# New lags and rates in the table that orders a hybrid DeltaNet and Conformer layer on one core

## The chip, the cores and the metric

The kernel runs on one core of a Trainium2 chip. A core has five engines that run side by side, each through its own queue of instructions in order: TensorE (PE, matrix products, with its weight loads PEld), VectorE (DVE), ScalarE (ACT), GpSimd (POOL) and SyncE (SP, which here only issues transfers). They wait for each other by semaphores. The metric is the device time of one execution in microseconds (us).

## The reference

One layer works on 256 latent tokens and 256 context tokens of width 2048, in fp32.

```
p  = h @ w_in           # latent tokens: q, k, v, beta/g, z, conformer a and gate
pc = hc @ w_in[:, :STATE_END]            # context tokens: k, v, beta/g are what counts
q, k, v = silu(depthwise_conv5(...)); q, k = l2_normalize(q), l2_normalize(k)
m     = strict_lower((k beta) k^T * decay);  t_inv = inverse(eye + m)     # per chunk
v_new = u - w @ state;  state = state * cd + k_dec^T @ v_new              # scan, both directions
mix = [rms_norm(o) * silu(z) , silu(layer_norm(depthwise_conv31(a * sigmoid(gate))))]
x   = x + g1 * rms_norm(mix @ w_out)
x   = x + g2 * rms_norm(swiglu(...))                                      # FFN
```

There are 8 heads of 128 columns, and the scans of the latent tokens start from the states that the context tokens leave.

## The kernel before

Each fp32 product is made of three products of rounded halves (hi by hi, lo by hi, hi by lo). Weights come in units of 512 KB into a ring of 4 (`raw`); ACT rounds a unit to `w_hi` (step `hi`, line 858) and DVE makes the rest `w_lo` (step `lo`, lines 1280 and 1247). A unit of `w_in` is used in two halves of 12 matmuls each (step `mm`, line 1700); this half is the beat of the program.

The program has three stages: modulation columns and first projections (up to about 130 us), the mixer (130 to 900 us), and the FFN (from there to the end). The mixer is written as one list of steps, `PLAN`, made by `make_plan`. Every engine walks the same list and takes the steps that are its own, so the list sets the order in every queue. In the skeleton of that list stand the halves of the projections in a fixed order (`STREAM`: for each pair of heads k and v of the context, a and g of the latent, later k, v, q, z of the latent). After each half the planner counts one slot on, and `beside` puts other steps in:

- three queues, `solve` (`solved`), `state` (`state_steps`) and `ready` (`keys_ready`, `queries_ready`). The head of a queue is placed when the steps that it names are at least so many slots back (`lag`); the tuple `(2, x)` reads "two slots after x". With an empty list it comes one slot after the chunk before it;
- `soon`: steps so many slots after the end of a projection (`evacuation`): the 5-tap convolution of k, v and q (`tap2` on ACT, `tapa` and `taps` on DVE, lines 973 and 1386), its SiLU (`csilu`, ACT, line 980), and its transpose (`nat`);
- `late`: the 31-tap convolution of a pair of channel tiles, 15 steps `dw` (DVE, line 1558, 4 instructions or more each), and behind the last of them the layer norm (`lnm`, `cen`, `lnv`, `lva`, `lnr`, `lnn`, `mix_lo`).

For each of eight pairs of heads (4 of the context, 4 of the latent) `solved` inverts a triangular matrix: `seed` (PE, line 1885) needs `yone` (DVE, writes `pi`, line 1431), then six levels of `z`, `zc`, `xy`, `xadd` (PE, ACT, PE, DVE: lines 1897, 858, 1907, 1444), the last `xadd` (DVE, writes `xyi`, line 1449), then a Newton step: `nr` (PE, lines 1916 and 1920) needs `xyi`, `nrr` (DVE, writes `zi`, line 1456), `nx` (PE, line 1928), `xf` (DVE, line 1469). `keys_ready` normalizes the keys (`kn`, DVE, line 1400) and transposes them (`kT`, PE, the helper line 1706, reads `kn`), makes decay factors (`dec`, `edec`) and the matrix (`gk`, `mneg`). `state_steps` runs the scan: `vn`, `vnc`, `st`, `ks`, `o`. The aux steps of PE share two PSUM banks: such a step waits until the reader of the one two before has taken its result away. `hi` and `lo` of later units are tied to the levels by `splits_ahead`: inside the solve `hi` follows `zc`, `lo` follows `xadd`.

Of the kernel before, what the change touches and what calls it, by code (L numbers as in the profile page):

```python
# [53 lines left out]
LEVELS = 7  # L54
# [13 lines left out]
GATE_STEPS = ["bac", "baT", "bsig", "ny", "nex", "nln", "gg", "pref", "eall", "nbe"]  # L68
# [6 lines left out]
PAIRS = [(CTX, p) for p in range(NP)] + [(LAT, p) for p in range(NP)]  # L75
# [4 lines left out]
def solved(m):  # L80

    s, p = PAIRS[m]
    old = [(*PAIRS[m - 1], t) for t in range(NT)] if m else []
    ch = []
    if m:
        ch = [([("nr", o) for o in old] + [("nrr", o) for o in old], [(2, ("xadd", (*PAIRS[m - 1], LEVELS - 1)))]), ([("nx", old[0])], [(1, ("nr", old[1]))]),
              ([("xf", old[0]), ("nx", old[1])], []), ([("xf", old[1])], [])]
    ch.append(([("yone", (s, p))], [(1, ("mk", (s, p, 0)))]))
    ch.append(([("seed", (s, p)), ("xadd", (s, p, 0)), ("mk", (s, p, 1))], []))
    for l in range(1, LEVELS):  # L90
        ch.append(([("z", (s, p, l))], [(2, ("xadd", (s, p, l - 1)))]))
        ch.append(([("zc", (s, p, l)), ("xy", (s, p, l)), ("xadd", (s, p, l))] + (
            [("mk", (s, p, l + 1))] if l + 1 < LEVELS else [("mlo", (s, p, t)) for t in range(NT)]), []))
    return ch

def last_solved():

    both = [(*PAIRS[-1], t) for t in range(NT)]
    return [([("nr", k) for k in both] + [("nrr", k) for k in both], [(2, ("xadd", (*PAIRS[-1], LEVELS - 1)))]), ([("nx", k) for k in both], [(1, ("nr", both[1]))]),  # L100
            ([("xf", k) for k in both], [])]

# [15 lines left out]
def queries_ready(p):  # L119

    t0, t1 = (LAT, p, 0), (LAT, p, 1)
    return [([("nsq", (LAT, "q", p)), ("nrt", (LAT, "q", p)), ("gm", (*t0, 1))], [(1, ("natc", ("q", LAT, p)))]),
            ([("nrc", (LAT, "q", p)), ("kn", (LAT, "q", p)), ("qdec", (p, 1))], []),
            ([("qT", (p, 0)), ("qTc", (p, 0)), ("dec", (*t0, 1)), ("edec", (*t0, 1)), ("gm", (*t1, 1))], [(2, ("kn", (LAT, "q", p)))] + (
                [(1, ("o", (p - 1,)))] if p else [])),
            ([("qT", (p, 1)), ("qTc", (p, 1)), ("qdec", (p, 2)), ("qk", (p, 0)), ("gq", (p, 0)), ("attn", (p, 0))], [(2, ("qT", (p, 0)))]),
            ([("dec", (*t1, 1)), ("edec", (*t1, 1)), ("qT", (p, 2)), ("qTc", (p, 2))], [(2, ("qT", (p, 1)))]),
            ([("qk", (p, 1)), ("gq", (p, 1)), ("attn", (p, 1))], [])]

def state_steps(m):

    s, p = PAIRS[m]
    ch = []
    for i in range(NT):
        first, last = (s == CTX and i == 0), (s == LAT and i == 1)
        ch.append(([("vb", (s, p, i))] + ([] if last else [("kd", (s, p, i))]) + (
            [] if first else [("ks", (s, p, i)), ("r", (s, p, i))]), [] if i else [(0, ("xf", (s, p, 1)))]))
        ch.append(([("vn", (s, p, i)), ("vnc", (s, p, i))], [(4, ("vb", (s, p, i)))]))
        if not last:  # L140
            ch.append(([("st", (s, p, i)), ("stc", (s, p, i))], [(2, ("vn", (s, p, i)))]))
    if s == LAT:
        ch.append(([("o", (p,)), ("oc", (p,)), ("osq", (p,)), ("ort", (p,))], [(1, ("attn", (p, 1)))]))
        ch.append(([("orc", (p,)), ("on", (p,))], [(3, ("o", (p,)))]))
        ch.append(([("oT", (p,)), ("ym", (p,)), ("mix_hi", (p,)), ("mix_lo", (p,))], [(2, ("on", (p,)))]))
    return ch

def norm_chunks():

    ch = [[("lnm", ()), ("cen", ())], [("csq", (0,))]]
    ch += [[("lnv", (i,)), ("lva", (i,))] + ([("csq", (i + 1,))] if i < 3 else []) for i in range(4)]
    ch += [[("lsd", ()), ("lnr", ()), ("lnn", ())]]
    ch += [[("lny", (i,)), ("mix_hi", (NP + i,)), ("mix_lo", (NP + i,))] for i in range(4)]
    return ch

def evacuation(cu):

    what, s, p = cu  # L160
    if what in "kvq":
        return [("tap2", cu), ("tapa", cu)], [(2, [("taps", cu)]), (6, [("csilu", cu)]), (6, [("nat", cu), ("natc", cu)])], []
    if what == "z":
        return [("zsilu", cu)], [], []
    if what == "a":
        return [], [], []
    return [("sg", (p,)), ("u", (p,))], [], [[("dw", (p, n))] for n in range(NDW)]
# [6 lines left out]
def turn_steps(q, s):  # L174

    return [(k, (s, kp)) for kp in range(4 * q, 4 * q + 4) for k in ("hf", "hhi", "hlo")]

def make_plan():
# [5 lines left out]
    def put(steps):  # L185
        plan.extend(steps)
        for x in steps:
            placed[x] = slot[0]

    def unit(u, halves=1, beside=lambda: None):  # L190
        plan.extend([("hi", (u,)), ("lo", (u,))])
        for half in range(halves):
            plan.append(("mm", (u, half)))
            beside()

    solve = [x for m in range(len(PAIRS)) for x in solved(m)] + last_solved()
    state = [x for m in range(len(PAIRS)) for x in state_steps(m)]
    ready = [x for m in range(NP + 1) for x in keys_ready(m)]
    for p in range(NP):
        ready += (keys_ready(NP + 1 + p) if p < NP - 1 else []) + queries_ready(p)  # L200
    queues = [solve, state, ready]
    since = [0, 0, 0]
    soon = []
    late = []
    slot = [0, 0, 0]

    def advance():

        slot[0] += 1
        for n, queue in enumerate(queues):  # L210
            if queue and slot[0] > since[n] and all(
                    x in placed and slot[0] - placed[x] >= lag for lag, x in queue[0][1]):
                put(queue.pop(0)[0])
                since[n] = slot[0]
# [9 lines left out]
    def beside():  # L224

        advance()
        if soon and slot[0] >= soon[0][0]:
            follow(soon.pop(0)[1])
        if late and (slot[0] % 2 == 1 or 1 * len(late) > slot[2] - slot[0]):
            put(late.pop(0))  # L230

    def follow(steps):
        for kind, key in steps:
            m = PAIRS.index(key[1:]) if kind == "nat" else 0
            if kind == "nat" and m >= (2 if key[0] in "kv" else NP + 2):
                s, p = PAIRS[m - 2]
                until({"k": ("st", (s, p, 1 if s == CTX else 0)), "v": ("vb", (s, p, 1)), "q": ("qT", (p, 2))}[key[0]])
        put(steps)

    def gates(n):  # L240
        for grp, j in mr[:n]:
            if grp and j == 0:
                plan.extend([("mcol", (grp - 1,)), ("mcc", (grp - 1,))])
            plan.append(("mrm", (grp, j)))
            if j == KT - 1:
                plan.append(("mrc", (grp,)))
        del mr[:n]
# [3 lines left out]
    for n in range(NMOD):  # L251
# [14 lines left out]
        if n >= NMOD // 2 + 4 and n % 2 == 0 and early:  # L266
            cu, g = early.pop(0)
# [6 lines left out]
    for n, cu in enumerate(STREAM):  # L274
        if cu == ("z", LAT, NP - 1):
            gates(len(mr))
            plan.extend([("mcol", (MR - 1,)), ("mcc", (MR - 1,))])
        rest = [c[0] for c in STREAM[n:]]
        slot[2] = slot[0] + 8 * (rest.index("g") + 1 if "g" in rest else 4)
        for g in range(2 if cu in EARLY else 0, 4):  # L280
            unit(("win", cu, g), 2, beside)
            done += 1
            gates(MR * KT * done // total - (MR * KT - len(mr)))
            if n == 0:
                plan.extend(turn_steps(1, LAT)[6 * (g - 2):6 * (g - 2) + 6])
        now, then, later = evacuation(cu)
        put(now)
        soon += [(slot[0] + wait, steps) for wait, steps in then]
        late += later
        if cu == ("g", LAT, 3):  # L290
            late += norm_chunks()
        if n in (1, 5):
            s = n // 4
            unit(("ba", s))
            put([(x, (s,)) for x in GATE_STEPS[:7]])
            soon.append((slot[0] + 7, [(x, (s,)) for x in GATE_STEPS[7:]]))
            soon.sort(key=lambda x: x[0])
    for c, kg in WO_FIRST:
        if kg < 4:
# [1790 lines left out]
```

## Time and profile before

| | us |
|---|---|
| median of 3 runs | 1712.98 |
| lowest, highest | 1710.34, 1717.55 |
| the profiled execution | 1717.55 |
| its span, first to last instruction | 1715.8 |
| PE busy | 1576.0 (92%) |
| DVE busy | 1040.8 (61%) |
| ACT busy | 769.3 (45%) |

Idle time in front of an instruction is put down to whoever ended it. From 900 us on the FFN keeps PE busy nearly all the time, and no step there is in the list that is changed.

### The profile page before, as it was taken

What the parts mean: (1) busy time and instruction counts of PE and PEld (TensorE: products, weight loads), DVE (VectorE), ACT (ScalarE), POOL (GpSimd) and SP (SyncE); (2) the same over time, 40 slices, a digit from 0 to 9 for tenths busy, and PEclk for the clock granted to TensorE, in tenths of its full rate; (3) what the DMA queues carried; (4) which work ended last, traced back from release to release, by engine and by line L of the source; (5) the groups of instructions that cost most, each with busy time, mean ns of one, the idle gap of its engine ahead of it and who ended that gap; (6) DMA issues with size and microseconds to landing.
All of it is one profiled execution on the core that took longest, in us unless ns stands there. A gap on an engine that the chain in (4) does not pass through costs nothing.

```text
span 1715.8 us, 25102 instructions
## 1 busy us (share of the span) xinstructions
PE 1576.0 (92%) x9317; PEld 1316.5 (77%) x9317; DVE 1040.8 (61%) x1436; ACT 769.3 (45%) x1036; POOL 222.0 (13%) x236
## 2 busy tenths in 40 slices
PE   4778889898989789999999799999999999999997
PEld 0356879787878788888878688888888888888785
DVE  1245888898798647575555645444545455677553
ACT  5435353434343654646544544444444444343332
POOL 2000222222222332424400000000000000000000
PEclk9899999899999999999999899999999999999999
DMA  9975535555554345464355366665656665988553
GB/s 360 400 283 168 176 130 196 169 170 166 172 177 156 124 146 192 141 206 151 113 182 193 101 191 190 188 192 185 193 185 190 188 188 178 328 315 311 211 181 114
DMA packets 182786, 334.58 MB, mean 195 GB/s; under 512 B 14707, under 2 KB 80355, under 8 KB 181794
## 3 DMA queue, kind: packets, MB, share of 16 engines
q1 hardware_dynamic: 182002, 330.89, 57.7%
q0 software_dynamic: 688, 2.39, 0.5%
q8 instruction: 63, 1.03, 0.2%
q14 instruction: 33, 0.26, 0.0%
HBM read 331.15 MB, written 2.10 MB: 194 GB/s over the span
## 4 chain that ended last, share of the span: by engine, by line
PE 74%; DVE 10%; DMA 6%; issue 5%; ACT 3%; POOL 1%; SPq 1%; DVEq 0%; ACTq 0%; POOLq 0%
PE PS L1700 61%; DMA first<-in_w_mod_dram 5%; DVE w_lo L1280 2%; DVE sil L1386 2%; PE PS L1907 2%; PE PS L1706 2%; DVE cacc L1558 2%; PE PS L1955 2%; PE PS L2000 2%; PE PS L1855 1%; PE PS L1897 1%; PE PS L1920 1%; DMA raw<-in_w_mod_dram 1%; PE PS L1793 1%; DVE mn L1420 1%
## 5 line engine op out<-in xcount | busy, mean ns | idle before, releaser
L858 ACT ACTIVATE w_hi<-raw 128x1024 fp32r<-128x1024 f32 x426 | 447.7, 1056 | 546.2 <-PE PS L1700 455.0
L1247 DVE TENSOR_TENSOR w_lo<-raw,w_hi 128x1024 fp32r<-128x1024 f32 x264 | 323.2, 1225 | 330.0 <-ACT w_hi L858 330.0
L1700 PE MATMUL PS<-w_hi,h_hi 128*128 128x512 f32 x704 | 274.8, 390 | 0.0
L1700 PE MATMUL PS<-w_hi,h_lo 128*128 128x512 f32 x704 | 274.0, 389 | 0.0
L1700 PE MATMUL PS<-w_lo,h_hi 128*128 128x512 f32 x704 | 274.0, 389 | 0.0
L1280 DVE TENSOR_TENSOR w_lo<-raw,w_hi 128x1024 fp32r<-128x1024 f32 x162 | 202.5, 1258 | 80.8 <-ACT w_hi L858 80.8
L1700 PE MATMUL PS<-h_hi,w_hi 128*128 128x256 f32 (+1 forms) x784 | 238.6, 304 | 2.3 <-DVE sil L1386 2.3
L1700 PE MATMUL PS<-h_lo,w_hi 128*128 128x256 f32 (+1 forms) x784 | 224.3, 286 | 0.0
L1700 PE MATMUL PS<-h_hi,w_lo 128*128 128x256 f32 (+1 forms) x784 | 224.0, 286 | 0.0
L1700 PEld LDWEIGHTS PS<-h_hi,w_hi 128*128 128x128 f32 (+1 forms) x784 | 151.5, 193 | 37.6 <-issue 30.9
L1700 PEld LDWEIGHTS PS<-w_hi,h_lo 128*128 128x128 f32 x704 | 132.1, 188 | 27.6
L1700 PEld LDWEIGHTS PS<-w_lo,h_hi 128*128 128x128 f32 x704 | 132.2, 188 | 27.1
L1700 PEld LDWEIGHTS PS<-w_hi,h_hi 128*128 128x128 f32 x704 | 132.2, 188 | 27.0
L1700 PEld LDWEIGHTS PS<-h_lo,w_hi 128*128 128x128 f32 (+1 forms) x784 | 151.8, 194 | 0.9
L1700 PEld LDWEIGHTS PS<-h_hi,w_lo 128*128 128x128 f32 (+1 forms) x784 | 151.3, 193 | 0.1
L1700 PE MATMUL PS<-w_hi,act_hi 128*128 128x512 f32 x352 | 140.4, 399 | 0.0
L1700 PE MATMUL PS<-w_hi,act_lo 128*128 128x512 f32 x352 | 139.5, 396 | 0.0
L1700 PE MATMUL PS<-w_lo,act_hi 128*128 128x512 f32 x352 | 139.5, 396 | 0.0
L1558 DVE SCALAR_TENSOR_TENSOR cacc<-ub,vcol,cacc 128x196 f32<-128x196 f32 (+14 forms) x240 | 121.1, 565 | 0.2
L807 POOL TENSOR_TENSOR mkl<-kc,lvl 128x512 fp32r<-128x512 f32 x56 | 78.8, 1408 | 170.3 <-PE PS L1897 159.3
L1700 PE MATMUL PS<-hc_hi,w_hi 128*128 128x256 f32 (+1 forms) x272 | 83.8, 308 | 11.7 <-DVE sil L1386 3.7
L1444 DVE TENSOR_TENSOR gh<-PS,side 128x1024 fp32r<-128x1024 f32 x48 | 58.6, 1221 | 52.2 <-PE PS L1907 49.8
(314 smaller groups left out, 2396.0 us busy)
## 6 DMA issues: line engine op xcount, KB each, us to landing
raw<-in_w_in_dram SPq DMA_DIRECT2D x128, 512.0 KB, 3.9
raw<-in_w_mod_dram SPq DMA_DIRECT2D x96, 512.0 KB, 5.1
raw<-in_w_gate_dram SPq DMA_DIRECT2D x88, 512.0 KB, 3.5
raw<-in_w_up_dram SPq DMA_DIRECT2D x88, 512.0 KB, 3.5
raw<-in_w_down_dram SPq DMA_DIRECT2D x88, 512.0 KB, 4.3
first<-in_w_mod_dram SPq DMA_DIRECT2D x64, 512.0 KB, 9.4
raw<-in_w_out_dram SPq DMA_DIRECT2D x32, 512.0 KB, 4.2
gin<-in_w_mod_dram SPq DMA_DIRECT2D x32, 512.0 KB, 5.5
```

The lines of the kernel that those rows point to most:

```text
L807: pool.tensor_tensor(mkl[:, :, :, :].rearrange("p t h c -> p (t h) c"), kc[:, :, :, :].bitcast(F32).rearrange("p t h c -> p (t h) c"), bc( ...
L858: act.activation(out_ap, in_ap, ACT.Copy).then_inc(S[kind], 1)
L1247: dve.tensor_tensor(w_lo[:, slot, :], raw[:, (R0 + n) % RING, :], w_hi[:, slot, :].bitcast(F32), ALU.subtract).then_inc(S["lo"], 1)
L1280: dve.tensor_tensor(lo, raw[:, at_ring[u] % RING, 0:sz], hi.bitcast(F32), ALU.subtract).then_inc(done, 1)
L1386: ins = dve.scalar_tensor_tensor(out=o, in0=pr[:, T * h + a + off:T * h + b + off], scalar=vcol[:, col:col + 1], in1=o, op0=ALU.mult, op1= ...
L1444: dve.tensor_tensor(gh[:, :, :, :, :].rearrange("p a t h c -> p (a t h) c"), grown.rearrange("p a (n c) -> p (a n) c", c=P), bc(side[:, l, ...
L1558: ins = dve.scalar_tensor_tensor(out=dst, in0=src, scalar=vcol[:, col:col + 1], in1=dst, op0=ALU.mult, op1=ALU.add)
L1700: ins = pe.matmul(out_ap, a[i], b[j], start=start and n == 0, stop=stop and n == 2, skip_group_check=grouped)
L1706: ins = pe.transpose(PS[:, bank_, P * n:P * (n + 1)], src, ident[:, :])
L1907: ins = pe.matmul(PS[:, b, P * n:P * (n + 1)], a, m, start=False, stop=True, skip_group_check=True)
L1955: ins = pe.matmul(PS[:, b, P * n:P * (n + 1)], a, m, start=True, stop=True)
L2000: ins = pe.matmul(PS[32 * tile:32 * tile + 1, 3, :], csil[:, LAT, j:j + 1], raw[:, n % RING, 512 * h:512 * (h + 1)], start=j == 0, stop=j ...
```

## The change

Six lags and two rates of the planner get other numbers. The step `nr` no longer asks for two slots behind the last `xadd`, and `nx` asks for two behind `nr` instead of one; the same in `last_solved`. The second transposition of the queries and `st` lose their lag. `on` asks for two slots behind `o` instead of three. `csilu` comes 4 slots behind the end of its projection instead of 6. The second half of the gate steps (`pref`, `eall`, `nbe`) comes 4 slots behind instead of 7. The `late` steps are placed in every slot, not in every second, once twice their number is more than the slots left. No computation is added or taken away, and the order of the weight transfers stays.

```
@@ solved, last_solved
-        ch = [([("nr", o) ...], [(2, ("xadd", (*PAIRS[m - 1], LEVELS - 1)))]), ([("nx", old[0])], [(1, ("nr", old[1]))]),
+        ch = [([("nr", o) ...], []), ([("nx", old[0])], [(2, ("nr", old[1]))]),
...
@@ queries_ready
-            ([("qT", (p, 1)), ("qTc", (p, 1)), ... ("attn", (p, 0))], [(2, ("qT", (p, 0)))]),
+            ([("qT", (p, 1)), ("qTc", (p, 1)), ... ("attn", (p, 0))], []),
@@ state_steps
-            ch.append(([("st", (s, p, i)), ("stc", (s, p, i))], [(2, ("vn", (s, p, i)))]))
+            ch.append(([("st", (s, p, i)), ("stc", (s, p, i))], []))
...
-        ch.append(([("orc", (p,)), ("on", (p,))], [(3, ("o", (p,)))]))
+        ch.append(([("orc", (p,)), ("on", (p,))], [(2, ("o", (p,)))]))
@@ evacuation
-        return [...], [(2, [("taps", cu)]), (6, [("csilu", cu)]), (6, [("nat", cu), ("natc", cu)])], []
+        return [...], [(2, [("taps", cu)]), (4, [("csilu", cu)]), (6, [("nat", cu), ("natc", cu)])], []
@@ make_plan
-        if late and (slot[0] % 2 == 1 or 1 * len(late) > slot[2] - slot[0]):
+        if late and (slot[0] % 2 == 1 or 2 * len(late) > slot[2] - slot[0]):
...
-            soon.append((slot[0] + 7, [(x, (s,)) for x in GATE_STEPS[7:]]))
+            soon.append((slot[0] + 4, [(x, (s,)) for x in GATE_STEPS[7:]]))
```

What it moves is seen in the queues. First DVE, from the last `xadd` of the second pair of heads (`xyi`) to the normalized keys of the third (`kn`). `cacc` is the 31-tap convolution, `sil` the 5-tap one, `zi` is `nrr`, `xf_ctx` is `xf`. Before:

```order
L1558 SCALAR_TENSOR_TENSOR cacc<-ub,vcol,cacc 128x4x59 x2
L1558 SCALAR_TENSOR_TENSOR cacc<-ub,vcol,cacc 128x4x60 x2
L1449 TENSOR_TENSOR xyi<-PS,tri 128x2x512 x2
L1280 TENSOR_TENSOR w_lo<-raw,w_hi 128x1024 x2
L1558 SCALAR_TENSOR_TENSOR cacc<-ub,vcol,cacc 128x4x61 x2
L1558 SCALAR_TENSOR_TENSOR cacc<-ub,vcol,cacc 128x4x62 x2
L1456 TENSOR_TENSOR zi<-PS,ident 128x512 x2
```

The same place now:

```order
L1449 TENSOR_TENSOR xyi<-PS,tri 128x2x512 x2
L1280 TENSOR_TENSOR w_lo<-raw,w_hi 128x1024
L1558 SCALAR_TENSOR_TENSOR cacc<-ub,vcol,cacc 128x4x59 x2
L1558 SCALAR_TENSOR_TENSOR cacc<-ub,vcol,cacc 128x4x60 x2
L1456 TENSOR_TENSOR zi<-PS,ident 128x512 x2
```

One step of the convolution that stood ahead of `xyi` now stands behind it. Some rows further on the keys stood behind the 5-tap convolution of the values; before:

```order
L1386 SCALAR_TENSOR_TENSOR sil<-PS,vcol,sil 128x254
L1280 TENSOR_TENSOR w_lo<-raw,w_hi 128x1024
L1469 TENSOR_TENSOR xf_ctx<-PS,xyi 128x512
L1394 RECIPROCAL rstd<-rtmp 128x4
L1400 TENSOR_TENSOR kn<-kn,rstd 128x512
```

and now they stand ahead of it:

```order
L1469 TENSOR_TENSOR xf_ctx<-PS,xyi 128x512
L1558 SCALAR_TENSOR_TENSOR cacc<-ub,vcol,cacc 128x4x63 x4
L1469 TENSOR_TENSOR xf_ctx<-PS,xyi 128x512
L1394 RECIPROCAL rstd<-rtmp 128x4
L1400 TENSOR_TENSOR kn<-kn,rstd 128x512
L1386 SCALAR_TENSOR_TENSOR sil<-PS,vcol,sil 128x254
```

The second place is DVE in the solve of the fourth pair of heads, where the last of the four 31-tap convolutions runs (from its fourth level to the next `xadd`, `gh`). Before there is one step `dw` (two rows) between `gh` and `gh` or two:

```order
L1444 TENSOR_TENSOR gh<-PS,side 128x1024
L1280 TENSOR_TENSOR w_lo<-raw,w_hi 128x1024
L1558 SCALAR_TENSOR_TENSOR cacc<-ub,vcol,cacc 128x4x53 x2
L1558 SCALAR_TENSOR_TENSOR cacc<-ub,vcol,cacc 128x4x54 x2
L1558 SCALAR_TENSOR_TENSOR cacc<-ub,vcol,cacc 128x4x55 x2
L1558 SCALAR_TENSOR_TENSOR cacc<-ub,vcol,cacc 128x4x56 x2
L1444 TENSOR_TENSOR gh<-PS,side 128x1024
```

and now there are three:

```order
L1444 TENSOR_TENSOR gh<-PS,side 128x1024
L1280 TENSOR_TENSOR w_lo<-raw,w_hi 128x1024
L1558 SCALAR_TENSOR_TENSOR cacc<-ub,vcol,cacc 128x4x55 x2
L1558 SCALAR_TENSOR_TENSOR cacc<-ub,vcol,cacc 128x4x56 x2
L1280 TENSOR_TENSOR w_lo<-raw,w_hi 128x1024
L1558 SCALAR_TENSOR_TENSOR cacc<-ub,vcol,cacc 128x4x57 x2
L1558 SCALAR_TENSOR_TENSOR cacc<-ub,vcol,cacc 128x4x58 x2
L1558 SCALAR_TENSOR_TENSOR cacc<-ub,vcol,cacc 128x4x59 x2
L1558 SCALAR_TENSOR_TENSOR cacc<-ub,vcol,cacc 128x4x60 x2
L1444 TENSOR_TENSOR gh<-PS,side 128x1024
```

The `late` steps of the fourth convolution end 12 slots earlier (slot 147, not 159), and the layer norm behind them with them.

## Rows read from the trace of the kernel before

**Rows 1.** The page's first and second part: busy us; granted clock in 40 slices.
```profile
PE 1576.0 (92%) x9317; PEld 1316.5 (77%) x9317; DVE 1040.8 (61%) x1436; ACT 769.3 (45%) x1036; POOL 222.0 (13%) x236
PEclk9899999899999999999999899999999999999999
```
**Rows 2.** Busy time, 130 to 900 us: PE, PEld, DVE, ACT, POOL, PEclk, DMA, GB/s.
```profile
130.00:900.00 770.00, 698.87 (x5239) 622.34 (x5238) 559.80 (x929) 371.24 (x575) 212.76 (x209) 0.96 0.50 163
```
**Rows 3.** Waits of PE, 130 to 900 us: total us, times, longest.
```profile
PE PS L1916 <- issue: 9.8, 3, 4.0
PE PS L1706 <- DVE kn L1400: 7.9, 6, 1.8
PE PS L1885 <- DVE pi L1431: 7.2, 5, 2.9
PE PS L1916 <- DVE e_ L1405: 6.0, 2, 4.0
...
PE PS L1872 <- ACT qTs L858: 2.3, 3, 0.8
```
**Rows 4.** Timeline of PE in the first pair: start, us, instruction [idle before].
```profile
152.26 0.66 PE L1706 MATMUL PS<-ident,sil 128*128 128x128 f32 x4 [1.67 <-ACT sil L980]
...
156.62 0.35 PE L1700 MATMUL PS<-h_hi,w_hi 128*128 128x256 f32 x1 [2.27 <-DVE sil L1386]
...
177.80 0.36 PE L1700 MATMUL PS<-hc_hi,w_hi 128*128 128x256 f32 x1 [2.49 <-DVE ub L1538]
```
**Rows 5.** The chain of waits, second pair's last level: start, us, what.
```profile
303.42 3.07 PE PS L1700 x24
306.49 3.30 issue
```
**Rows 6.** Timeline of DVE at the same place.
```profile
305.83 1.59 DVE L1558 SCALAR_TENSOR_TENSOR cacc<-ub,vcol,cacc 128x236 f32<-128x236 f32 x4
307.34 2.35 DVE L1449 TENSOR_TENSOR xyi<-PS,tri 128x1024 fp32r<-128x1024 f32 x2
```
**Rows 7.** Timeline of DVE and PE at the third pair's keys.
```profile
322.89 2.04 DVE L1386 SCALAR_TENSOR_TENSOR sil<-PS,vcol,sil 128x254 f32<-128x254 f32 x4 [3.69 <-ACT sil L973]
...
326.78 0.69 DVE L1400 TENSOR_TENSOR kn<-kn,rstd 128x512 f32<-128x512 f32 x1
...
327.53 0.66 PE L1706 MATMUL PS<-ident,kn 128*128 128x128 f32 x4 [1.38 <-DVE kn L1400]
```
**Rows 8.** The same engines at the fourth pair's seed.
```profile
429.10 2.53 DVE L1558 SCALAR_TENSOR_TENSOR cacc<-ub,vcol,cacc 128x224 f32<-128x224 f32 x4
431.56 0.67 DVE L1431 SCALAR_TENSOR_TENSOR pi<-mkl,nid_r 128x512 fp32r<-128x512 f32 x1
...
432.28 1.11 PE L1885 MATMUL PS<-nid_r,pi 128*128 128x128 f32 x4 [2.85 <-DVE pi L1431]
```
**Rows 9.** Busy time of all engines in two stretches of the fourth convolution.
```profile
454.30:504.70 50.40, 44.47 (x351) 39.89 (x351) 45.36 (x75) 21.67 (x34) 13.56 (x13) 0.97 0.54 178
504.70:541.00 36.30, 34.11 (x255) 31.04 (x254) 33.62 (x64) 13.85 (x20) 10.54 (x9) 0.95 0.51 164
```
**Rows 10.** Busy time of line 1558 alone in the same: DVE, PEclk, DMA, GB/s.
```profile
454.30:504.70 50.40, 18.00 (x36) 0.97 0.54 178
504.70:541.00 36.30, 11.84 (x24) 0.95 0.51 164
```
**Rows 11.** Timeline of DVE and PE at the fifth pair's last level.
```profile
577.71 1.75 DVE L1579 RECIPROCAL cx<-cx 128x256 f32<-128x256 f32 x1
579.49 2.29 DVE L1582 TENSOR_TENSOR cacc<-cacc,cx 128x2048 f32<-128x2048 f32 x1
...
582.26 0.77 PE L1916 MATMUL PS<-xyi,nid_r 128*128 128x512 f32 x1 [4.00 <-DVE e_ L1405]
```
**Rows 12.** Busy time around two long waits of PE.
```profile
308.00:319.00 11.00, 9.21 (x42) 9.05 (x42) 9.98 (x16) 1.44 (x2) 0.00 (x0) 0.53 0.62 200
...
581.00:589.00 8.00, 6.74 (x31) 6.57 (x32) 4.87 (x9) 3.51 (x6) 0.00 (x0) 0.57 0.24 68
```

More of the change, by code:

```diff
@@ L85, in solved @@
     if m:
-        ch = [([("nr", o) for o in old] + [("nrr", o) for o in old], [(2, ("xadd", (*PAIRS[m - 1], LEVELS - 1)))]), ([("nx", old[0])], [(1, ("nr", old[1]))]),
+        ch = [([("nr", o) for o in old] + [("nrr", o) for o in old], []), ([("nx", old[0])], [(2, ("nr", old[1]))]),
               ([("xf", old[0]), ("nx", old[1])], []), ([("xf", old[1])], [])]
@@ L99, in last_solved @@
     both = [(*PAIRS[-1], t) for t in range(NT)]
-    return [([("nr", k) for k in both] + [("nrr", k) for k in both], [(2, ("xadd", (*PAIRS[-1], LEVELS - 1)))]), ([("nx", k) for k in both], [(1, ("nr", both[1]))]),
+    return [([("nr", k) for k in both] + [("nrr", k) for k in both], []), ([("nx", k) for k in both], [(2, ("nr", both[1]))]),
             ([("xf", k) for k in both], [])]
@@ L125, in queries_ready @@
                 [(1, ("o", (p - 1,)))] if p else [])),
-            ([("qT", (p, 1)), ("qTc", (p, 1)), ("qdec", (p, 2)), ("qk", (p, 0)), ("gq", (p, 0)), ("attn", (p, 0))], [(2, ("qT", (p, 0)))]),
+            ([("qT", (p, 1)), ("qTc", (p, 1)), ("qdec", (p, 2)), ("qk", (p, 0)), ("gq", (p, 0)), ("attn", (p, 0))], []),
             ([("dec", (*t1, 1)), ("edec", (*t1, 1)), ("qT", (p, 2)), ("qTc", (p, 2))], [(2, ("qT", (p, 1)))]),
@@ L161, in evacuation @@
     if what in "kvq":
-        return [("tap2", cu), ("tapa", cu)], [(2, [("taps", cu)]), (6, [("csilu", cu)]), (6, [("nat", cu), ("natc", cu)])], []
+        return [("tap2", cu), ("tapa", cu)], [(2, [("taps", cu)]), (4, [("csilu", cu)]), (6, [("nat", cu), ("natc", cu)])], []
     if what == "z":
```

## The prediction

> **What bounds the kernel now.** First the page: PE is busy 1576.0 us of the 1715.8, 92%, and the next engine, DVE, 61% [rows 1]. The slices say where the rest is: up to slice 22 or so, about 950 us, the granted clock dips to 8 tenths now and then; later it hardly does [rows 1]. The steps that the change touches all lie in the mixer, so I asked for the busy time from 130 to 900 us: PE 698.87 of 770 us, so 71 us idle, and a mean clock of 0.96 [rows 2]. With two levels, 1.2 and 2.4 GHz, 0.04 missing means 8% of the stretch, 62 us, at the lower one, and half of that, about 31 us, is lost to it. These 71 and 31 us, 102 together, are all that an order can win here; the work is the same before and after. Then the waits of PE in that stretch: PE waits mostly for DVE, a few us at a time [rows 3]. The line 1916 rows are `nr` after the last level, 9.8 and 6.0 us in five waits; the trace names "issue" or `e_` as releaser, but `nr` needs `xyi`, and the timeline shows it: `xyi` (307.34, 2.35 us) ends at 309.7, and the wait that began at 306.49 and lasted 3.30 us ends at 309.8 [rows 5, 6]. `xyi` itself was late because DVE had a convolution step of 1.59 us ahead of it [rows 6]. So what counts is in which order DVE takes its work where it has a backlog, and how much PE work stands between a step and its reader.
>
> **The start (pairs one and two).** Three waits of PE: 1.67 us for the SiLU of the first keys, 2.27 us for `taps`, 2.49 us for `u` [rows 4]. `csilu` two slots earlier is done before the first gate steps on ACT, so the 1.67 us go; what is late next is `taps` of the values, which DVE starts about 0.7 us earlier, so of the 2.27 us wait 1 us more is waited (the 1.67 us saved only bring PE there earlier): gain 1.0. The early `pref` (1.4 us of PE, moved from behind the matrix to ahead of it) lets `mneg`, POOL's `kc` and `seed` come about 2.5 us earlier; `u` follows its projection instead of `yone`. Gain 2. Together **-3**, between 0 and -6.4 (all three waits gone).
>
> **Keys.** `kT` waits for `kn` six times, 7.9 us [rows 3]. At the third pair DVE takes `tapa` (2.04 us, itself 3.69 us late), `lo` and `xf` ahead of `kn`; `kT` starts 0.06 us after `kn` ends [rows 7]. In the new order `kn` stands ahead of that `tapa`, so it is some 4 to 5 us earlier, while `kT` moves only one slot, about 2.8 us with its aux work. These waits vanish where DVE has the keys' norms in time; one of the six lies in the stretch priced below (1.5 us). Of the other 6.4 us I take **-5.5**; bounds 0 and -6.4.
>
> **Seeds.** Five waits for `pi`, 7.2 us [rows 3]. At the fourth pair DVE did 2.53 us of convolution ahead of `pi` [rows 8]; now `yone` stands ahead of that step, and `seed` moves one slot. 2.53 against one half of 1.53 us (24 matmuls 3.07 us, so 12 take 1.53 [rows 5]): about 1 us per pair plus what the faster `mneg` gives. Four pairs: **-3.5**; bounds +1 and -7.2.
>
> **The Newton step.** `nr` moves one slot ahead relative to its level, so PE has one half, 1.53 us, less to do before it. DVE gives `xyi` earlier by the step that now stands behind it, 1.59 us at the second pair [rows 6], nothing at the first. `nx` keeps its place, so no new wait after it. At the first pair `kk` stands right behind `nr` and needs its bank, which `nrr` frees only after `lo`, `taps` and `lo` on DVE: a new wait, from 0 to 3 us. Four pairs with a wait now: 4 x 1.53 = 6.1 against about 3 won: **+3**; bounds -2 and +9. Behind the waiting `nr` are all products of PE; ACT and DVE then idle for their next projection (the 3.69 us in [rows 7]).
>
> **The fourth convolution.** Its 15 steps take 18.00 us (36 instructions, 9 steps) in 454 to 505 us and 11.84 us (6 steps) in 505 to 541 us [rows 10]. All 15 now fall into the first stretch, where DVE was already busy 45.36 of 50.4 us [rows 9]: 45.4 + 11.8 = 57.2 us, 6.8 us more than the stretch has. PE waits for it at `z` of the fifth level and at `nr`. Add 1.2 us for the sums over channels, which need a bank there: **+8**; bounds +2 (if PE's own idle time and low clock in the stretch, about 7 us, take it up) and +11.
>
> **Where it is given back.** At the fifth pair DVE did the reciprocal and the scaling of the layer norm, 1.75 + 2.29 us, right ahead of `nr`'s needs, and PE waited 4.00 us, then ran at a clock of 0.57 for 8 us [rows 11, 12]: at 0.57, 6.9 of 8 us at 1.2 GHz, 3.4 us lost. Now the norm is done before. The wait, the 3.4 us, and 1.6 us of small waits of the norm's own steps and of `mix_lo`, 9.0 in all; one new bank wait of about 1 us behind `nr`: **-8**; bounds 0 and -10.
>
> **The rest.** The second transposition of queries: three waits of `qk` for `qTc`, 2.3 us in all [rows 3]; the new order has a `dec` and a transposition next to each other in their place: **+1**, bounds -2 and +5. `st` right behind `vn`, `on` and the later `pref` cost nothing: one half of PE, 1.53 us, covers the copy between. The clock: by [rows 12] a wait of 3.30 us was followed by 11 us at 0.53, so each long wait that goes or comes takes 2 to 5 us with it. I count one such stretch less (the seed of the fourth pair): **-3**; bounds -6 and +5.
>
> The sum: -3 - 5.5 - 3.5 + 3 + 8 - 8 + 1 - 3 = -11 us, from 1717.55 us of the profiled execution to 1706.5. That execution lies 4.6 us over the median of 1712.98; the same difference from the median gives 1702. I take 1703, since the small waits are most likely to leave a remainder.
>
> **A rule against it.** In the trace a wait of 4.00 us is followed by a stretch at 0.57, one of 3.30 us by 0.53 [rows 11, 12], while the waits of 1.67 and 1.38 us have no such row. The Trainium skill, "TensorE: Matmul & The Clock Gate", section "HAM oscillation — how this bites in real kernels", says in substance that the clock is lost to gaps that are long, not to the sum of gaps. The trace agrees so far. By that rule the long waits, not their total, are what to count, and it is weighed as the first rival.
>
> **Rivals.** (1) *Short waits go, long ones grow, no change.* What goes is mostly below 2 us; the four waits at `nr` are the long ones, and each loses 1.53 us of cover. If DVE's earlier `xyi` does not make that up, 4 x 1.53 = 6.1 us come, and one more low stretch of 3.4 us; with 8 for the convolution and 1 for the rest 18.5, against 3 + 5.5 + 3.5 + 8 = 20: -1.5 us, 1711. For it: the wait at `nr` ends by `xyi` on a DVE busy 43 to 46 of 50 us. Against it: the step of 1.59 us moved behind.
> (2) *Slower: the convolution's backlog.* The place is 454 to 505 us. Its price is the 8 us above, up to 11, if PE there stalls twice in long waits; it decides if the time is not given back at 582 us because the wait there only moves (the keys' `kk` now stands right behind `nr` and needs `nrr`). Then 11 + 3 (`nr`) + 3.4 (a low stretch at the long wait) + 1 = 18.4 against 3 + 3 + 2 = 8 for what is left of start, keys and seeds: +10, 1723.
> (3) *All short waits go.* Start -6.4, keys -6.4, seeds -7.2, `nr` 0, convolution +6, given back -9, clock -3, rest 0: -26; half of the extra, since the waits follow each other: -20, 1693.
> That the steps don't move is excluded by the new order of the queues.
>
> **How the numbers follow.** Forecast 1703, own range 1697 to 1709: 0.45. Rival 1 (1711): 0.22. Rival 2 (1723): 0.18. Rival 3 (1693): 0.15. What a measurement can tell from no change is about 0.5%, 8.6 us, so below 1704.4 is faster and above 1721.5 slower. Of the forecast three quarters are faster (0.34); rival 3 is faster (0.15), rival 1 one tenth (0.02): 0.51. Rival 2 lies around the upper bound, two thirds of it (0.12) beyond. The rest, 0.37, is the same. I write 0.50, 0.36, 0.14. The range: 1691 to 1721, which leaves out a part of rivals 2 and 3.
>
> **What would show it.** Right: in the waits of PE the row for `kn` falls from 7.9 to below 3 us and that for `pi` below 4; PE idles more between 454 and 505 us, with `cacc` steps back to back on DVE; no wait of 4 us and no low clock near 575 us; idle time of PE from 130 to 900 us falls from 71 to 60 to 65 us. Wrong: if `nr` waits 5 us or more at three pairs, if the mean clock in the mixer is below 0.96, if ACT waits for `taps` in front of `csilu` and holds up `zc` or `hi` (a wait of ACT that the rows before don't show), or if the time lost near 480 us is still missing at 600 us.

## The result, and the profile after

The changed kernel takes 1760.02 us (median of 4, 1754.59 to 1764.38) against 1713.35 us before (4, 1710.34 to 1717.55): ratio 1.0269, 95% interval 1.023 to 1.0308. It is 2.7% slower, 46.7 us. The forecast was 1703, the range ended at 1721.

The page and the busy time of the same work, from 130 us to where the FFN begins, now 941 instead of 900 us (PE, PEld, DVE, ACT, POOL, PEclk, DMA, GB/s), against [rows 1, 2]:

```profile
PE 1585.4 (90%) x9317; PEld 1324.2 (75%) x9317; DVE 1040.9 (59%) x1436; ACT 765.2 (44%) x1034; POOL 222.8 (13%) x236
...
PEclk9899989898989899999999899999999999999999
```

```profile
130.00:941.00 811.00, 710.26 (x5227) 629.85 (x5227) 560.31 (x929) 367.29 (x573) 213.49 (x209) 0.94 0.48 155
```

DVE, ACT and POOL are as busy as before to within 5 us: the work is the same. PE idles 811 - 710.26 = 100.7 us instead of 71.1, so +29.6; and it is busy 11.4 us longer, with a mean clock of 0.94 instead of 0.96. These two make the 41 us by which the stretch is longer; the FFN has none of it. So of the difference between these two traces 7 in 10 are waits and 3 in 10 the clock. The two profiled executions (1757.66 and 1717.55 us) lie 40.1 us apart, the medians 46.7: the last 6.6 us these traces don't show. The waits of PE, against [rows 3]:

```profile
PE PS L1916 <- issue: 20.9, 6, 9.1
PE PS L1885 <- DVE pi L1431: 13.6, 6, 4.4
PE PS L1907 <- ACT pi L858: 8.9, 4, 3.4
PE PS L1700 <- DVE sil L1386: 7.7, 2, 5.0
PE PS L2000 <- DMA raw<-in_w_mod_dram: 5.7, 4, 1.8
PE PS L1864 <- DVE zi L1456: 4.8, 2, 2.4
```

`nr` (L1916) waits 20.9 instead of 15.8 us, `kk` (L1864, the products of the keys, behind it in PE's row) 4.8 more, `seed` 13.6 instead of 7.2, `xy` for `zc` on ACT 8.9 instead of 2.5. Only the keys are better: `kT` for `kn` has 1.8 us in two waits instead of 7.9.

The longest wait stands where the fourth convolution was moved to. DVE, PE and ACT in the timeline (start, us, instruction [idle before]):

```profile
480.93 1.21 DVE L1280 TENSOR_TENSOR w_lo<-raw,w_hi 128x1024 fp32r<-128x1024 f32 x1
482.06 6.70 DVE L1558 SCALAR_TENSOR_TENSOR cacc<-ub,vcol,cacc 128x244 f32<-128x244 f32 x8
488.68 2.02 DVE L1386 SCALAR_TENSOR_TENSOR sil<-PS,vcol,sil 128x254 f32<-128x254 f32 x4
490.62 1.62 DVE L1558 SCALAR_TENSOR_TENSOR cacc<-ub,vcol,cacc 128x248 f32<-128x248 f32 x4
492.16 2.35 DVE L1449 TENSOR_TENSOR xyi<-PS,tri 128x1024 fp32r<-128x1024 f32 x2
...
494.61 0.77 PE L1916 MATMUL PS<-xyi,nid_r 128*128 128x512 f32 x1 [9.07 <-issue]
...
497.67 1.28 ACT L980 ACT_TABLE_LOAD   x1 [9.36 <-DVE sil L1386]
```

The products that `xyi` reads (L1907) were done at 484.1 and PE's last half at 485.5, where PE stops, but DVE had 6.70 + 2.02 + 1.62 us of convolutions in its row ahead of it. ACT stands at `csilu` for 9.36 us through the same backlog. What PE paid for it, busy time from 483 to 502 us:

```profile
483.00:502.00 19.00, 9.93 (x56) 9.15 (x59) 18.75 (x32) 4.35 (x5) 4.70 (x6) 0.64 0.37 115
```

DVE works 18.75 of 19 us, PE 9.93, and the clock is 0.64.

### The profile page after: what moved, and what is told of

Read it like the earlier page. It is cut to its first block, busy times and chain, and to the rows that moved or that the text cites. A ratio compares the mean times of both kernels' runs of the same rounds, so it can differ in the third digit from the quotient of the medians.

```text
span 1755.9 us, 25100 instructions
## 1 busy us (share of the span) xinstructions
PE 1585.4 (90%) x9317; PEld 1324.2 (75%) x9317; DVE 1040.9 (59%) x1436; ACT 765.2 (44%) x1034; POOL 222.8 (13%) x236
## 4 chain that ended last, share of the span: by engine, by line
PE 73%; DVE 10%; issue 6%; DMA 6%; ACT 3%; POOL 2%; SPq 0%; DVEq 0%; ACTq 0%; POOLq 0%
PE PS L1700 60%; DMA first<-in_w_mod_dram 4%; DVE cacc L1558 3%; DVE w_lo L1280 2%; PE PS L1907 2%; PE PS L1955 2%; PE PS L2000 2%; PE PS L1706 2%; DVE sil L1386 1%; DMA raw<-in_w_mod_dram 1%; PE PS L1855 1%; PE PS L1897 1%; PE PS L1793 1%; POOL kc L795 1%; PE PS L1920 1%
## 5 line engine op out<-in xcount | busy, mean ns | idle before, releaser
L1700 PE MATMUL PS<-h_hi,w_hi 128*128 128x256 f32 (+1 forms) x784 | 242.3, 309 | 2.7 <-DVE sil L1386 2.7
L1700 PEld LDWEIGHTS PS<-h_hi,w_hi 128*128 128x128 f32 (+1 forms) x784 | 155.6, 198 | 39.1 <-issue 36.5
```

Of the source, the lines that this page charges most:

```text
L1700: ins = pe.matmul(out_ap, a[i], b[j], start=start and n == 0, stop=stop and n == 2, skip_group_check=grouped)
```

## The experiments

Twelve kernels, each with the times of before taken beside it. All ratios are to the kernel before. Where a text below speaks of half 137 or half 169, the halves of the projections are counted from the first on, a unit of the gates as one; "behind" means that this half starts later than in the trace of the kernel before. That trace is itself 4.6 us above the median, so differences of a few us against it are weak, and the column on the right is what counts.

| kernel | ratio | 95% | difference of the medians, us |
|---|---|---|---|
| changed kernel | 1.0269 | 1.023 to 1.0308 | +46.7 |
| rate of `late` alone | 1.0036 | 1.0022 to 1.0049 | +6.3 |
| `nr`, `nx` alone | 1.0082 | 1.0067 to 1.0096 | +14.5 |
| `csilu` alone | 1.0049 | 1.0036 to 1.0062 | +8.4 |
| the four other lags | 1.0129 | 1.0115 to 1.0144 | +21.3 |
| of these, queries alone | 1.0027 | 1.0016 to 1.0038 | +5.4 |
| gate steps alone | 1.0037 | 1.0025 to 1.005 | +7.0 |
| `st` alone | 1.0042 | 1.003 to 1.0054 | +6.6 |
| `on` alone | 0.9994 | 0.9985 to 1.0002 | -1.7 |
| `csilu` moved, chain not | 1.0039 | 1.0026 to 1.0052 | +5.9 |
| `nr` one slot later | 0.9998 | 0.9989 to 1.0006 | +0.2 |
| rate at 1.25 | 1.0014 | 1.0003 to 1.0025 | +2.0 |
| all but the rate | 1.0244 | 1.023 to 1.0259 | +40.4 |

### The four groups, each alone

**The rate.**

```
-        if late and (slot[0] % 2 == 1 or 1 * len(late) > slot[2] - slot[0]):
+        if late and (slot[0] % 2 == 1 or 2 * len(late) > slot[2] - slot[0]):
```

> Only the rate of the late steps is changed (twice their number instead of once); all lags as before. Theory A (the convolution's backlog): in the changed kernel DVE took 10 us of convolution and 5-tap work ahead of the last xadd and PE waited 9.07 us at nr; from the half 141 to the half 157 it lost 12 us on the kernel before. If the rate alone does that, this kernel is 8 to 13 us slower than before, less the 4 us wait at the fifth pair (582 us) that goes: ratio 1.003 to 1.007, with a wait at nr of the fourth pair above 6 us. Theory B (csilu): the rate does little by itself, since the backlog hurts only where csilu stands right behind taps and holds up ACT: ratio 1.000 +- 0.002, nr of the fourth pair waits below 5 us.

Measured 1.0036: theory A's price. The wait at `nr` of the fourth pair is 5.5 us, a little under its 6. The halves of the projections, as they start in the timeline, show the course: level with before at half 137, 14.9 us behind at half 169, 5.2 us behind at half 185. The give-back is there: `nr` of the fifth pair waits 0.1 instead of 4.0 us, and its low clock is gone. From 575 to 589 us PE was busy 10.0 of 14 us at a clock of 0.76 before, and here

```profile
575.00:589.00 14.00, 11.49 (x92) 10.11 (x91) 10.42 (x15) 11.71 (x25) 6.14 (x7) 1.00 0.49 161
```

The same work lies some 10 us later here, so the 18 us around that `nr` are the fairer pair: 578 to 596 us before, PE busy 12.8 at 0.81; 584 to 602 us here, 15.9 at 1.00.

**The Newton step.** The edit is that of `solved` and `last_solved` in the diff above.

> Only nr (lag 2 behind the last xadd gone) and nx (2 behind nr instead of 1). Theory C (the Newton step has lost its cover): nr stands one slot, 1.53 us of PE, nearer to xadd at all eight pairs; at the four or five with a wait already 1.5 us more each, at the others a wait of up to 1 us, each long one with a low clock behind it: 8 to 15 us slower, ratio 1.005 to 1.009. Theory B (csilu): nr alone costs at most what it wins at DVE, 0 to 5 us: ratio 1.000 to 1.003, and the 20.9 us of waits at nr in the changed kernel come from DVE's work being late for other reasons.

Measured 1.0082: theory C. Its waits, and `kk`'s behind `nr`:

```profile
PE PS L1916 <- issue: 23.4, 7, 6.6
...
PE PS L1864 <- DVE zi L1456: 3.3, 1, 3.3
...
PE PS L1916 <- POOL mlo L814: 1.0, 1, 1.0
```

24.4 + 3.3 against 15.8 us: 11.9 of the 14.5 us. Pair by pair `nr` goes 1.97 to 2.85, 3.30 to 4.75, 3.97 to 5.41, 2.50 to 6.57 us, the fifth 4.00 to 1.25 with 3.33 at `kk` behind it, and three pairs that had none wait 1.0 to 1.6. The second pair, DVE and PE:

```profile
306.02 2.02 DVE L1386 SCALAR_TENSOR_TENSOR sil<-PS,vcol,sil 128x254 f32<-128x254 f32 x4
307.97 1.59 DVE L1558 SCALAR_TENSOR_TENSOR cacc<-ub,vcol,cacc 128x236 f32<-128x236 f32 x4
309.48 2.35 DVE L1449 TENSOR_TENSOR xyi<-PS,tri 128x1024 fp32r<-128x1024 f32 x2
...
311.92 0.77 PE L1916 MATMUL PS<-xyi,nid_r 128*128 128x512 f32 x1 [4.75 <-issue]
```

Against [rows 6] the step of 1.59 us still stands ahead of `xyi`: this lag takes cover from PE and gives nothing to DVE. `nr` and `nx` were moved together; no run separates them.

**csilu.**

```
-        ... (6, [("csilu", cu)]), (6, [("nat", cu), ("natc", cu)])], []
+        ... (4, [("csilu", cu)]), (6, [("nat", cu), ("natc", cu)])], []
```

The planner places one chunk of `soon` in a slot, so `nat`, the keys and the whole solve follow one slot earlier.

> Only csilu 4 slots behind the projection instead of 6; nat, the keys and the whole solve follow it one slot earlier. Theory B: in the changed kernel ACT waits at csilu for taps 28.7 us in seven places (9.36 the longest; 1.1 us in three places before), with zc and hi behind it; that is the main cost: 18 to 30 us slower than before, ratio 1.010 to 1.018, with ACT's waits for taps above 15 us. Theory A or C: the waits at csilu are a result of DVE's backlog, which the rate and nr make; by itself csilu costs 0 to 6 us, ratio 0.998 to 1.004, with waits of ACT for taps below 10 us.

Measured 1.0049. The mechanism is theory B's (ACT waits 33.9 us for the 5-tap convolution), the price is not: 8.4 us, not 18 to 30. Most of ACT's waiting is hidden. In the waits of PE `kT` has 2.0 us left of 7.9, and `nr` of the second pair waits 1.62 instead of 3.30; but `seed` waits 12.9 instead of 7.2, and `kk`, which now meets a busy DVE, 5.2.

**The other four lags.** The remaining edits of the diff: queries, `st`, `on`, gate steps.

> Only the second transposition of queries, st, on and the gate steps (four lags), which my prediction took as worth nothing to +1 us. If that holds: ratio 0.998 to 1.002. Rival (the scan is the cost): qk, vn, o and st in the latent pairs wait more in the changed kernel (zd of 3.2 and 2.2 us at qk, 2.0 at st, 3.5 at the first transposition of the FFN's columns), from 600 to 900 us it lost 18 us on the kernel before; then this one is 8 to 15 us slower, ratio 1.005 to 1.009, nearly all of it behind 600 us.

Measured 1.0129, the largest of the four, where my prediction had +1 us. The rival's range, 8 to 15 us, is passed as well; its place, behind 600 us, holds for the larger part: from the starts of the halves this kernel is 6 us behind already at half 57 (the gates), 4 at half 177 (590 us before), 8 to 9 at 209 and 19 at 265. The parts multiply to 1.0036 x 1.0082 x 1.0049 x 1.0129 = 1.0299 against 1.0269: nearly a plain sum.

### The four lags, one by one

> Of the four lags of the run before (1.0129), only that of the second transposition of queries. Theory D (order on ACT): the queries' products come one slot earlier, and with them o of the second and third pair, whose scaling and the q norms on ACT (822.88 to 826.7 us there) then stand ahead of zc of the fourth level, for which PE waited 1.52 and 3.01 us; and qTc of the last pair stands behind mix_hi (PE waits 3.23 us): 8 to 12 us slower, ratio 1.005 to 1.007, all of it behind the half 209, with a wait of xy for ACT above 1 us there. Theory E (the scan's copies): st right behind vn is what costs; the queries alone do -2 to +3 us, ratio 0.999 to 1.002.

```
-            ([("qT", (p, 1)), ("qTc", (p, 1)), ... ("attn", (p, 0))], [(2, ("qT", (p, 0)))]),
+            ([("qT", (p, 1)), ("qTc", (p, 1)), ... ("attn", (p, 0))], []),
```

Measured 1.0027: theory D's place at half its price. `o` of the third pair comes one slot earlier, and its followers stand on ACT ahead of `zc` of the fourth level:

```profile
809.91 0.60 ACT L858 ACTIVATE rb<-PS 128x512 f32<-128x512 f32 x1 [4.28 <-PE PS L1971]
810.53 1.28 ACT L1083 ACT_TABLE_LOAD   x1
...
813.49 0.30 ACT L1009 ACTIVATE rtmp<-sums,cst 128x4 f32<-128x4 f32 x1
813.69 0.58 ACT L858 ACTIVATE pi<-PS 128x512 fp32r<-128x512 f32 x1
...
814.32 0.48 PE L1907 MATMUL PS<-pi,gh 128*128 128x128 f32 x1 [3.01 <-ACT pi L858]
```

From the copy of `o` to `zc` are 3.8 us of table load, square root and norms; before, `zc` was ahead of them and `xy` waited for nothing. The wait of 3.23 us at `qk` (L1872) is not here but only with all four lags: it needs `on` moved as well, whose `mix_hi` then stands ahead of `qTc` on ACT. That is an interaction, some 3 us, and part of why these four sum to 1.0100 and together give 1.0129.

> Only the second half of the gate steps 4 slots after the first instead of 7. In the run with four lags PE lost 6 us from the half 53 to the half 57: pref now stands between xyi and nr and waits for DVE (1.72 us), and two stretches at the lower clock follow each other. If the gate steps alone do that: 4 to 7 us slower behind the half 57, ratio 1.002 to 1.004. If it came of st or of chance: within 2 us, ratio 0.999 to 1.001.

```
-            soon.append((slot[0] + 7, [(x, (s,)) for x in GATE_STEPS[7:]]))
+            soon.append((slot[0] + 4, [(x, (s,)) for x in GATE_STEPS[7:]]))
```

Measured 1.0037. `pref` of the second gate group, first in PE's row between `xyi` and `nr`, waits 2.98 us where `nr` waited 1.97, and the second pair's `seed`, with no wait before, waits 1.32:

```profile
237.54 1.59 DVE L1558 SCALAR_TENSOR_TENSOR cacc<-ub,vcol,cacc 128x240 f32<-128x240 f32 x4
239.05 0.41 DVE L1405 TENSOR_TENSOR e_<-PS,e_ 128x256 f32<-128x256 f32 x1
...
239.61 0.59 PE L1826 MATMUL PS<-g,tri 128*128 128x16 f32 x4 [2.98 <-DVE e_ L1405]
```

By the profile it waits for `gk` (`e_`) to empty a bank, and DVE has a convolution step ahead of that. These waits are 2.3 us; the rest of the 7.0 I can't place. The profiled execution of this kernel (1718.96 us) lies only 1.4 us above that of before (1717.55), so its trace has no more to show.

> Only st without its lag behind vn (and what follows it one slot earlier, o of the first and the last pair with it). Theory E: the scan is the cost of the four lags, 8 us or more, ratio 1.005 or above, with waits at st or vn. Theory D: 1 to 4 us, ratio 1.0005 to 1.0025, from the seeds, which find DVE busy with the scan (seed of the third and fourth latent pair waits 2.0 and 1.8 us there, 0 and 0.8 before).

```
-            ch.append(([("st", (s, p, i)), ("stc", (s, p, i))], [(2, ("vn", (s, p, i)))]))
+            ch.append(([("st", (s, p, i)), ("stc", (s, p, i))], []))
```

Measured 1.0042, between the two. The waits are at `seed`, as theory D had it: 12.6 us in seven against 7.2 in five. At the seventh pair (DVE, then PE) the state `slat` now comes ahead of `mneg` (`mn`), from which `kc`, `mk` and `pi` follow; before it came behind:

```profile
687.66 1.12 DVE L1499 SCALAR_TENSOR_TENSOR slat<-sctx,ex,PS 128x128 f32<-128x128 f32 x4 [1.90 <-PE PS L1955]
688.71 0.60 DVE L1420 SCALAR_TENSOR_TENSOR mn<-e_,nbeta,m_gt 128x128 f32<-128x128 f32 x2
...
694.56 0.69 DVE L1431 SCALAR_TENSOR_TENSOR pi<-mkl,nid_r 128x512 fp32r<-128x512 f32 x1 [1.50 <-POOL mkl L807]
```

DVE has nothing else to do before `slat` for 1.90 us, in which it could have made `mn`: it waits at the head of its queue for PE.

> Only on 2 slots behind o instead of 3, four times. My prediction took it as nothing: ratio 0.999 to 1.001. Rival: on (1.3 us of DVE) and its transposition come ahead of the last levels' splits, and DVE's lo or ACT's hi come late for zc: 2 to 4 us, ratio 1.001 to 1.0025. Theory D has 0 here and all of qk's 3.23 us in the queries' run.

```
-        ch.append(([("orc", (p,)), ("on", (p,))], [(3, ("o", (p,)))]))
+        ch.append(([("orc", (p,)), ("on", (p,))], [(2, ("o", (p,)))]))
```

Measured 0.9994 with an interval that holds 1: nothing, as predicted. It is the only one of the seven edits that costs nothing by itself.

### What separates the theories

> csilu 4 slots behind the projection as in the run with csilu alone (1.0049), but nat asks for 7: so csilu alone moves, and the transposition, keys and solve keep their slots. Theory B (ACT stands at csilu): in that run ACT waited some 34 us for taps in ten places. If that is what costs, this kernel is as slow, ratio 1.004 or more. Theory F (the chain of keys and solve, one slot earlier, meets DVE with its work unfinished: seeds waited 12.9 us instead of 7.2, kk and nx 9 us more): the wait on ACT is hidden, ratio 0.998 to 1.001.

```
-        ... (6, [("csilu", cu)]), (6, [("nat", cu), ("natc", cu)])], []
+        ... (4, [("csilu", cu)]), (7, [("nat", cu), ("natc", cu)])], []
```

Measured 1.0039: theory B, and F falls. Only `csilu` moved, and some three quarters of its cost are there (5.9 of 8.4 us); the earlier chain of keys and solve adds the rest. The place in which it is seen, first ACT, then PE:

```profile
203.68 1.28 ACT L980 ACT_TABLE_LOAD   x1 [5.61 <-DVE sil L1386]
...
205.50 0.58 ACT L858 ACTIVATE pi<-PS 128x512 fp32r<-128x512 f32 x1
...
206.14 0.48 PE L1907 MATMUL PS<-pi,gh 128*128 128x128 f32 x1 [2.98 <-ACT pi L858]
```

ACT stands 5.61 us at `csilu`, `zc` comes behind its table load, and `xy` waits 2.98 us. The wait on ACT is 23.1 us in this trace (1.1 before), and PE's waits grow by a fraction of it.

> The opposite direction: nr asks for 3 slots behind the last xadd instead of 2 (nx and all behind it later with it, a slot or two). Theory C (cover): each of the five waits at nr before (1.97, 3.30, 3.97, 2.50, 4.00 us, 15.8 in all) has 1.5 us more work of PE in front of it and shrinks by that: nr waits some 8 us, the time is 3 to 8 us shorter, ratio 0.995 to 0.998. Rival G: two slots are the optimum; what nr waits less, the seed, the values' scan and the state behind it wait more: ratio 0.999 to 1.003.

```
-        ... [(2, ("xadd", (*PAIRS[m - 1], LEVELS - 1)))]) ...     (and in last_solved)
+        ... [(3, ("xadd", (*PAIRS[m - 1], LEVELS - 1)))]) ...
```

Measured 0.9998: rival G. `nr` has one wait of 1.5 us left, and others have taken the place of its waits (`pref` is L1826, `dec` L1855), whose longest are 4.7 us at `pref`, 4.0 at `kk` and 3.0 at `dec`:

```profile
PE PS L1826 <- DVE xf_ctx L1469: 4.7, 1, 4.7
PE PS L1928 <- DVE zi L1456: 4.5, 3, 2.0
PE PS L1864 <- DVE e_ L1405: 4.3, 2, 4.0
...
PE PS L1855 <- DVE xf_ctx L1469: 3.0, 1, 3.0
```

So a slot of cover less (with `nx` moved too) costs 14 us, and one more wins nothing.

> The rate of the late steps at 1.25 times their number instead of once (twice cost 1.0036): the fourth convolution ends 6 slots earlier instead of 12. Twice lost 15 us from the half 137 to 169 and gave 8 back at the layer norm (the 4 us wait at nr of the fifth pair and its low clock). If the two can be had apart, this loses at most 5 us and gives 4 to 8 back: ratio 0.997 to 1.000. Rival: the layer norm now falls ahead of nr or the seed of the fifth pair in another way, or the loss grows with the first steps that move: 1.001 to 1.003.

```
-        if late and (slot[0] % 2 == 1 or 1 * len(late) > slot[2] - slot[0]):
+        if late and (slot[0] % 2 == 1 or 5 * len(late) > 4 * (slot[2] - slot[0])):
```

Measured 1.0014 (1.0003 to 1.0025): a small loss, within the rival's range and above the other's. In its trace the two nearly cancel: 4.8 us are lost from half 137 to 157 and 5.4 given back to half 185. No rate was found that gives back more than it costs.

> The changed kernel with the rate left as before. If the parts add up (the rate alone 1.0036, the whole 1.0269): 1.0233, within 0.002. Rival: in the changed kernel the rate's loss of 12 us between the halves 141 and 157 is not given back (it was 25.4 us behind at the half 169, 22.0 at 177), because ACT stands 9.36 us at csilu behind the same convolution: then leaving it out wins 10 us or more, ratio 1.017 to 1.021.

Measured 1.0244: the parts add up, the rival falls. The rate is worth 0.25% in the changed kernel and 0.36% alone; it is not what ruins it. The traces show the same course inside the changed kernel: against this one it falls behind by 14.9 us from half 137 to 169 and gets 8.5 back by half 185.

No kernel was found that beats the one before by more than the measurement can tell. Not tried: `csilu` at 5, and any order in which POOL's steps are kept away from the convolution (see the last section).

## Why the prediction was wrong

**Start, -3.** Not confirmed. In the changed kernel the halves between the two units of the gates (135.9 to 212.9 us before) take 73.6 us instead of 77.1. But the kernel before and seven of the others (rate, `nr`, queries, `st`, `on`, `nr` later, rate at 1.25) have one and the same program there, and their traces take 73.2 to 77.5 us. The 3.5 us can't be told from this spread.

**Keys, -5.5.** Right for this wait: `kT` waits 6.1 us less.

**Seeds, -3.5.** Wrong by its sign: +6.4 us. I gave `yone` the convolution step that went behind it and forgot that `seed` ends a chain over three engines, `mneg` (DVE), `kc` and `mk` (POOL), `yone` (DVE). PE comes a slot earlier to a chain that is no faster: with `csilu` alone, which moves that chain, `seed` waits 12.9 us (9.1 with `csilu` moved and the chain not), with `st` alone 12.6. At the fourth pair, DVE, PE and POOL, against [rows 8]:

```profile
432.31 1.55 DVE L1558 SCALAR_TENSOR_TENSOR cacc<-ub,vcol,cacc 128x232 f32<-128x232 f32 x4
433.79 1.21 DVE L1280 TENSOR_TENSOR w_lo<-raw,w_hi 128x1024 fp32r<-128x1024 f32 x1
437.49 0.69 DVE L1431 SCALAR_TENSOR_TENSOR pi<-mkl,nid_r 128x512 fp32r<-128x512 f32 x1 [2.49 <-POOL mkl L807]
...
438.24 0.69 PE L1885 MATMUL PS<-nid_r,pi 128*128 128x128 f32 x2 [4.37 <-DVE pi L1431]
...
432.47 3.65 POOL L795 TENSOR_TENSOR kc<-mn 128x512 fp32r<-128x512 f32 x1 [7.18 <-DVE mn L1420]
```

The convolution is no longer what holds up `pi`: DVE waits there 2.49 us for POOL, whose `kc` takes 3.65 us where it took 2.2 before.

**The Newton step, +3.** 14.5 us, 11.5 more than my term. The lost cover of 1.53 us a pair was about right at the first three pairs (0.9, 1.5 and 1.4 us), and three further pairs began to wait. But I set against them DVE's step of 1.59 us, which is won by the `csilu` edit and not by this one, and even with it the second pair waits 5.47 us in the changed kernel against 3.30 before. And I had no term for `nr`'s own followers: while PE stands at `nr`, nothing behind it runs, so ACT and DVE get their next work later. That this is why `nr` of the fourth pair grew from 2.50 to 6.57 us is my reading; no run shows it. The bound of +9 was too low as well.

**The fourth convolution, +8, and the give-back, -8.** The give-back was right: 9.7 us from half 169 to 185 with the rate alone. The loss was 15 us in the trace, about twice my term, and the two together cost 6.3 us by the medians, where I had nothing. I took the loss from the total of DVE's work over 50 us, while PE waits for the step that is behind the densest piece.

**The rest, +1.** The term that failed most: +21.3 us, where I allowed +5 at most for the queries and nothing for the others. I looked for the cost of each of these steps on PE, found a half of cover, 1.53 us, and called it nothing. The cost was at what they displace: `zc` behind the norms on ACT, `mn` behind the state on DVE, `nr` behind `pref`.

**csilu.** My list of signs had it (ACT waits for `taps` ahead of `csilu` and holds up `zc`), the sum had not. It is 23.2 + 5.5 us of waiting on ACT in the changed kernel:

```profile
ACT L980 <- DVE sil L1386: 23.2, 6, 9.4
...
ACT sil L980 <- DVE sil L1386: 5.5, 1, 5.5
```

and by the run in which only it moved costs 5.9 us, with the chain behind it 8.4.

**The clock, -3.** Wrong sign, +11 us of busy time. By the rule of the Trainium skill that I weighed ("TensorE: Matmul & The Clock Gate", "HAM oscillation — how this bites in real kernels"), the long gaps decide; the trace agrees for the gap of 9.07 us (0.64 over 19 us), but waits of 3 us did not spare the clock either: after `xy`'s 3.03 us at 573.8

```profile
573.00:581.00 8.00, 7.16 (x37) 7.16 (x38) 5.12 (x6) 4.81 (x8) 0.00 (x0) 0.57 0.17 46
```

the clock is 0.57 over the next 8 us. Here the measurement decides against the rule as I put it; whether that one wait alone brought the clock down or the shorter idle times before it did their part, no run separates.

Of my signs of being wrong two came whole, the mean clock of 0.94 and ACT's waits for `taps`, and one in part, the time lost near 480 us. The side of rival 2 came true, a slower kernel, and so did its mechanism in part: what is lost at the wait for the fourth convolution is not all given back. But its price, 10 us, was a fifth of the real one, and of the 46.7 us the convolution explains 6.3. The real case, that each of six edits costs 5 to 15 us and that they add up (46.5 us as a plain sum of the seven, 46.7 together), was in none of my cases.

## What to carry to other kernels

In a table that orders in-order queues, a lag is cover: before you count what a step gains by standing earlier, read on each engine what it now stands ahead of, and whether its own input is there. An instruction that waits at the head of a queue holds up all that is behind it, and a sum over 50 us of an engine's work says nothing about the one step that somebody waits for. Seven small edits were tried at once here (six of lags, `nr` and `nx` counted as one, and one of a rate; the diff has no second rate); each alone showed in one run what the whole hid, and only one of them was free.

## What the runs showed of the hardware

**DVE and POOL slow each other.** The steps of the 31-tap convolution read two operands in SBUF. Of the 240 in the kernel before, the 186 that POOL's steps overlap for less than a quarter of their time take 0.41 to 0.48 us, mean 0.445; the 42 that POOL's steps overlap for more than three quarters take 1.1 us in the mean, up to 1.50. In the backlog that caused the wait of 9.07 us, eight of them took 6.70 us, where eight undisturbed ones are 8 x 0.445 = 3.6, while POOL ran

```profile
481.83 2.89 POOL L814 TENSOR_TENSOR mlo<-mn,mhi 128x512 fp32r<-128x512 f32 x2 [6.45 <-PE PS L1897]
484.68 1.52 POOL L828 TENSOR_TENSOR rb<-vn,beta 128x256 f32<-128x256 f32 x2
```

POOL's own instructions grow as well: `kc`, 3.65 us above, took 2.2 us at seven of the eight pairs before and 1.27 at the other. So 3 of the 9.07 us may be this. The Trainium skill, "SBUF — State Buffer", section "SBUF: two separate sides", has a port pair that DVE and GpSimd take from each other for a whole instruction, also where DVE reads two inputs from SBUF; the trace agrees: the first six of the eight take 1.51, 1.50, 0.82, 0.82, 0.71 and 0.82 us beside POOL's 1.47, 1.45 and four of 0.78. No run took POOL's steps away, so the share in the wait stays an estimate.

**A profile's own noise.** The eight kernels whose program is the same in the stretch from 135.9 to 212.9 us spread over 73.2 to 77.5 us there, at a granted clock of 0.94 to 0.98. A term of 3 us read from one trace of this kernel is not a finding; the medians over several runs were.
